# Moving one-hot products, GELU pairs and U steps in the first gate-table build of a one-core decoder trunk

## The reference

```python
q = (xn @ w_query).reshape(b, s, PEER_HEADS, 2, PEER_HALF)            # 8 heads, two halves of 128
sc = einsum('bshcd,hcnd->bshcn', q, sub_keys)                         # 128 keys per half
top_s, top_i = top_k(sc, 16)
best_s, best_pos = top_k(all 256 sums of two halves, 16)
expert_idx = top_i[..., 0] * 128 + top_i[..., 1]   # at best_pos
gates = softmax(best_s)
u = expert_u[ib]                                    # 128 experts of 1024 per token
act = gelu(einsum('ced,cd->ce', u, xb))
out = einsum('ce,ced->cd', gb * act, expert_v[ib])
```

## Time and profile before

| | |
|---|---|
| median of 3 runs | 2051.42 us (2044.77 to 2053.69) |
| the profiled execution | 2048.59 us, its span 2046.8 us |
| busy share of the span | PE 94%, DVE 59%, POOL 43%, ACT 20% |
| bytes moved | 613.47 MB, mean 300 GB/s |
| TensorE clock granted, mean | 0.96 of 2.4 GHz |

### The profile page before, as it was taken

How to read it: one execution, slowest core, us unless ns; L and a number is a source line. 1 busy time by engine, 2 the same in 40 slices (tenths; PEclk the granted TensorE clock), 3 DMA queues, 4 the chain that set the end, 5 groups by cost and what they waited for, 6 DMA issues and landing times.

```text
span 2046.8 us, 23875 instructions
## 1 busy us (share of the span) xinstructions
PE 1929.5 (94%) x8967; PEld 1246.4 (61%) x8967; DVE 1206.0 (59%) x3046; ACT 413.6 (20%) x963; POOL 878.3 (43%) x785
## 2 busy tenths in 40 slices
PE   8999999999989999999996789999999999999998
PEld 7688886956766787885675765444445543333332
DVE  1022101103968888889899999887777775444321
ACT  2233210111202454111211222000022320101102
POOL 0000000000855324445558355745566776666653
PEclk9999999999999999999998578999998999999999
DMA  7533444434999877999999587999998999999997
GB/s 236 151 117 114 146 153 145 143 108 137 378 334 397 282 250 251 379 386 379 332 358 387 192 264 241 409 409 409 409 384 321 347 332 405 409 409 409 409 382 285
DMA packets 252439, 613.47 MB, mean 300 GB/s; under 512 B 18676, under 2 KB 121124, under 8 KB 252324
## 3 DMA queue, kind: packets, MB, share of 16 engines
q0 software_dynamic: 110592, 402.70, 52.4%
q1 hardware_dynamic: 141120, 208.17, 29.4%
q10 hardware_dynamic: 612, 1.07, 0.2%
HBM read 609.77 MB, written 2.10 MB: 299 GB/s over the span
## 4 chain that ended last, share of the span: by engine, by line
PE 62%; DVE 13%; DMA 12%; POOL 7%; issue 3%; ACT 1%; another core or an unknown queue 1%; SPq 0%; DVEq 0%; ACTq 0%; POOLq 0%
PE ps L612 25%; PE ps L878 10%; PE ps L841 9%; DMA u_rows<-in_peer_u_dram,idx 8%; PE ps L627 7%; DVE u_rows L1353 5%; POOL u_rows L571 5%; PE ps L654 3%; PE ps L868 2%; POOL v_rows L585 2%; DMA wring<-in_w_branch_attn_dram 2%; DVE hot_a L1407 2%; DMA v_rows<-in_peer_v_dram,idx_turned 1%; DMA wring<-in_w_in_dram 1%
## 5 line engine op out<-in xcount | busy, mean ns | idle before, releaser
L571 POOL DMA_INDIRECT u_rows<-in_peer_u_dram,idx x512 | 591.5, 1155 | 979.0 <-DVE idx L1340 507.8
L1353 DVE CUSTOM_DVE_ANT_0 u_rows<-u_rows,xn 128x1024 f32<-128x1024 f32 x512 | 623.0, 1217 | 171.5 <-DMA u_rows<-in_peer_u_dram,idx 154.3
L612 PE MATMUL ps<-xT,wring 128*128 128x256 f32 x2432 | 552.7, 386 | 19.0 <-DMA wring<-in_w_in_dram 10.0
L612 PEld LDWEIGHTS ps<-xT,wring 128*128 128x128 f32 x2432 | 462.7, 193 | 87.8 <-DMA wring<-in_w_in_dram 10.8
L878 PE MATMUL ps<-d_rows,gates 128*128 128x512 f32 x1024 | 455.4, 598 | 0.5 <-issue 0.5
L878 PEld LDWEIGHTS ps<-d_rows,gates 128*128 128x128 f32 x1024 | 189.7, 190 | 265.2 <-issue 263.6
L841 PE MATMUL ps<-v_rows,diag 64*64 64x512 f32 x1928 | 260.0, 631 | 12.9 <-DMA v_rows<-in_peer_v_dram,idx_turned 7.9
L868 PEld LDWEIGHTS ps<-hot_b,hot_a 128*128 128x128 f32 x1024 | 148.2, 230 | 71.1 <-DVE hot_b L1415 36.5
L585 POOL DMA_INDIRECT v_rows<-in_peer_v_dram,idx x121 | 136.0, 1124 | 126.2 <-PE ps L841 92.3
L868 PE MATMUL ps<-hot_b,hot_a 128*128 128x64 f32 x1024 | 157.2, 318 | 33.4 <-DVE hot_b L1415 26.8
L841 PEld LDWEIGHTS ps<-v_rows,diag 64*64 64x64 f32 x1928 | 72.3, 138 | 158.5 <-issue 150.8
(11 more groups left out here) (197 smaller groups left out, 1701.2 us busy)
## 6 DMA issues: line engine op xcount, KB each, us to landing
wring<-in_w_in_dram SPq DMA_DIRECT2D x128, 512.0 KB
d_rows<-in_peer_v_dram SPq DMA_DIRECT2D x128, 512.0 KB
wring<-in_peer_w_query_dram SPq DMA_DIRECT2D x32, 512.0 KB
wring<-in_w_branch_conv_dram SPq DMA_DIRECT2D x16, 512.0 KB
wring<-in_w_branch_attn_dram SPq DMA_DIRECT2D x16, 512.0 KB
wring<-in_w_out_dram SPq DMA_DIRECT2D x16, 512.0 KB
wring<-in_xattn_wq_dram SPq DMA_DIRECT2D x16, 512.0 KB
wring<-in_xattn_wo_dram SPq DMA_DIRECT2D x16, 512.0 KB
```

The lines of the kernel that those rows point to most:

```text
L571: pool.indirect_dma_start(out=u_rows[:, n % URING, :], out_offset=None, in_=peer_u[0], in_offset=bass.IndirectOffsetOnAxis(ap=experts_of(g ...
L612: mm = pe.matmul(bank(job)[:, 0:HN], w[:, k % 4, P * b:P * (b + 1)], act[:, k, :], start=(k == 0), stop=(k == KT - 1))
L1353: dve.tensor_tensor_reduce(out=u, in0=u, in1=(xn2 if h else xn1)[:, i, :], scale=1.0, scalar=0.0, op0=ALU.mult, op1=ALU.add, accum_out=dot ...
```

## The change

The first 32 chunks stood in steps 268 to 302 (one to a step), with 22 V rows in steps 280 to 302. They now stand in steps 268 to 278, three to a step, with no V row. The blocks of the first half of the table stand in steps 281 to 390 (before 304 to 405), the second build in 392 to 427 with 76 V rows (before 407 to 433 with 84), and the steps up to 512 hold 140 V rows (before 110). In the first build `hot_a` of the ten chunks 2, 5, ..., 29 is written by ACT in two operations instead of by DVE: eight times the absolute value of the difference of iota and key, then relu of one minus it. The GELU chains of the groups 2k and 2k + 1 of half 0 run as one chain on 32 columns. `keep_running` lets PE repeat 4, 12 and 4 products of 128x512, whose result nobody reads, around the transposes of the tables.

```diff
-    CH_SLOT = spread(12, 46, 32) + spread(151, 177, 32)
-    BLK_SLOT = spread(48, 149, 64) + spread(179, 260, 64)
-    V_SLOT = (spread(24, 46, 22) + spread(48, 150, 14) + spread(151, 177, 84) + spread(179, 256, 110)
-              + spread(256, 280, 26))
+    CH_SLOT = spread(12, 23, 32) + spread(136, 171, 32)
+    BY_ACT = range(2, 32, 3)
+    BLK_SLOT = spread(25, 134, 64) + spread(173, 260, 64)
+    V_SLOT = spread(60, 134, 14) + spread(136, 171, 76) + spread(173, 256, 140) + spread(256, 280, 26)
-    ADD_SLOT = HSTEPS + 150
+    ADD_SLOT = HSTEPS + 135
+    def chain_of(g):
+        return g // 2 if g < HG else g - HG // 2
...
-        gl = tiny("gl", [P, 4, TOPK])
+        gl = tiny("gl", [P, 4, 2 * TOPK])
...
+            def keep_running(count):
+
+                for _ in range(count):
+                    pe.matmul(ps[:, 3, :], ident[:, :], xn2[:, 0, 0:BANK], start=True, stop=True)
+
             def table_transposes():
-                pe.wait_ge(wgt_rdy, HG)
+                pe.wait_ge(wt_done, 2 * SBH)
+                pe.wait_ge(x3_done, 2 * HT)
+                keep_running(4)
                 for b in range(NJB):
                     wait_taken(pe, NJOBS - 1 - b)
                 for i in range(HT):
                     for c in range(2):
-                        pe.transpose(ps[:, 6, P * (2 * i + c):P * (2 * i + c + 1)], e12[:, i, c, :], ident[:, :])
+                        mm = pe.transpose(ps[:, 6, P * (2 * i + c):P * (2 * i + c + 1)], e12[:, i, c, :], ident[:, :])
+                mm.then_inc(t_done, 1)
+                keep_running(12)
+                pe.wait_ge(wgt_rdy, HG)
                 for i in range(HT):
                     mm = pe.transpose(ps[:, 7, P * i:P * (i + 1)], wst[:, i, :], ident[:, :])
                 mm.then_inc(t_done, 1)
+                keep_running(4)
 
             def gate_chunk(ch):
                 pe.wait_ge(hot_rdy, ch + 1)
+                if ch in BY_ACT:
+                    pe.wait_ge(hot_steps, 2 * (BY_ACT.index(ch) + 1))
...
+            def first_hots(ch):
+                n = BY_ACT.index(ch)
+                i, o = 8 * ch // P, 8 * ch % P
+                if n == 0:
+                    act.wait_ge(t_out, 3)
+                    act.wait_ge(iotas, 2)
+                act.wait_ge(wb_done, ch - 1)
+                for t in range(8):
+                    ab = act.activation(hot_a[:, 8 * (ch % 2) + t, :], iota_a[:, :], ACT.Abs, scale=-1.0,
+                                        bias=e1T[:, i, o + t:o + t + 1])
+                ab.then_inc(hot_steps, 1)
+                act.wait_ge(hot_steps, 2 * n + 1)
+                a = hot_a[:, 8 * (ch % 2):8 * (ch % 2) + 8, :]
+                act.activation(a, a, ACT.Relu, scale=-1.0, bias=1.0).then_inc(hot_steps, 1)
...
-                if e == 5 and 0 < g <= GROUPS:
+                if e == 5 and 0 < g <= GROUPS and (g > HG or g % 2 == 0):
                     gelu_exp(g - 1)
...
+                for ch in BY_ACT:
+                    if CH_SLOT[ch] == tau:
+                        first_hots(ch)
                 for ch in range(CHUNKS):
                     if CH_SLOT[ch] + 1 == tau:
                         take_gates(ch)
...
-                dve.tensor_tensor(hot_a[:, 8 * (ch % 2):8 * (ch % 2) + 8, :],
-                                  e1T[:, i, o:o + 8].unsqueeze(2).to_broadcast([P, 8, P]),
-                                  iota_a[:, :].unsqueeze(1).to_broadcast([P, 8, P]), ALU.is_equal)
+                if ch not in BY_ACT:
+                    dve.tensor_tensor(hot_a[:, 8 * (ch % 2):8 * (ch % 2) + 8, :],
+                                      e1T[:, i, o:o + 8].unsqueeze(2).to_broadcast([P, 8, P]),
+                                      iota_a[:, :].unsqueeze(1).to_broadcast([P, 8, P]), ALU.is_equal)
```

More of the change, by code:

```diff
@@ L1060, in gelu_exp @@
             def gelu_exp(g):
-                act.wait_ge(gl_done, 7 * g + 4)
-                act.activation(gl[:, 2, :], gl[:, 1, :], ACT.Exp, scale=-GELU_C).then_inc(gle_done, 1)
+                n = TOPK * (1 + (g < HG))
+                act.wait_ge(gl_done, 7 * chain_of(g) + 4)
+                act.activation(gl[:, 2, 0:n], gl[:, 1, 0:n], ACT.Exp, scale=-GELU_C).then_inc(gle_done, 1)
             def diagonal(m):
@@ L1358, in gelu @@
                 hd, i, h = group(g)
-                r = g % GRING
-                a = dots[:, r, :]
-                n = 7 * g
+                first, wide = g - (1 - h), 2 - h
+                r = first % GRING
+                a = dots[:, r:r + wide, :]
+                s0, s1, s2, s3 = (gl[:, k, 0:wide * TOPK].rearrange("p (w e) -> p w e", w=wide) for k in range(4))
+                n = 7 * chain_of(g)
                 if part == 0:
                     dve.wait_ge(u_used, TOPK * (g + 1))
-                    dve.tensor_tensor(gl[:, 0, :], a, a, ALU.mult).then_inc(gl_done, 1)
+                    dve.tensor_tensor(s0, a, a, ALU.mult).then_inc(gl_done, 1)
@@ L1365, in gelu @@
                 elif part == 1:
                     dve.wait_ge(gl_done, n + 1)
-                    dve.tensor_scalar(gl[:, 0, :], gl[:, 0, :], 0.044715, 1.0, ALU.mult, ALU.add).then_inc(gl_done, 1)
+                    dve.tensor_scalar(s0, s0, 0.044715, 1.0, ALU.mult, ALU.add).then_inc(gl_done, 1)
                 elif part == 2:
                     dve.wait_ge(gl_done, n + 2)
-                    dve.tensor_tensor(gl[:, 1, :], gl[:, 0, :], a, ALU.mult).then_inc(gl_done, 1)
+                    dve.tensor_tensor(s1, s0, a, ALU.mult).then_inc(gl_done, 1)
@@ L1378, in gelu @@
+                    dve.reciprocal(gate_r[:, 0:wide], gate_s[:, r:r + wide]).then_inc(gl_done, 1)
                 elif part == 5:
-                    dve.wait_ge(gle_done, g + 1)
-                    dve.tensor_scalar(gl[:, 2, :], gl[:, 2, :], 1.0, None, ALU.add).then_inc(gl_done, 1)
+                    dve.wait_ge(gle_done, chain_of(g) + 1)
+                    dve.tensor_scalar(s2, s2, 1.0, None, ALU.add).then_inc(gl_done, 1)
                 elif part == 6:
                     dve.wait_ge(gl_done, n + 6)
-                    dve.reciprocal(gl[:, 2, :], gl[:, 2, :]).then_inc(gl_done, 1)
+                    dve.reciprocal(s2, s2).then_inc(gl_done, 1)
@@ L1386, in gelu @@
                     if h == 0:
-                        dve.scalar_tensor_tensor(out=wst[:, i, TOPK * hd:TOPK * (hd + 1)], in0=gl[:, 3, :],
-                                                 scalar=gate_r[:, g % 2:g % 2 + 1], in1=gl[:, 2, :],
-                                                 op0=ALU.mult, op1=ALU.mult).then_inc(wgt_rdy, 1)
+                        for k in range(HT):
+                            dve.scalar_tensor_tensor(out=wst[:, k, TOPK * hd:TOPK * (hd + 1)], in0=s3[:, k, :],
+                                                     scalar=gate_r[:, k:k + 1], in1=s2[:, k, :],
+                                                     op0=ALU.mult, op1=ALU.mult).then_inc(wgt_rdy, 1)
                     else:
@@ L1392, in gelu @@
                             to, a3, a2 = (t[:, k, :].rearrange("p (e two) -> p e two", two=2)[:, :, odd]
[L1393 removed]
+                                          for t, k in ((wgt, g - HG), (s3, 0), (s2, 0)))
                             ins = dve.scalar_tensor_tensor(out=to[p0.start + turn:p0.stop + turn, :], in0=a3[p0, :],
[L1395 removed]
+                                                           scalar=gate_r[p0, 0:1], in1=a2[p0, :],
                                                            op0=ALU.mult, op1=ALU.mult)
@@ L1458, in _ @@
                     dot(tau)
-                if 0 < g <= GROUPS and e < 8:
+                if 0 < g <= GROUPS and e < 8 and (g > HG or g % 2 == 0):
                     gelu(g - 1, e)
```

7 lines of the change are left out of this document (4 added, 3 removed).

## The result

The changed kernel takes 2111.23 us (median of 4 runs, 2108.27 to 2116.16) where the kernel before takes 2048.17 us (median of 4) beside it: ratio 1.0304, 95% interval 1.0274 to 1.0333. It is slower by 3%. The profiled execution took 2108.27 us, its span 2106.5 us.

A forecast was written before the change was run, and what follows sets the result against it. The prediction took transfers at 409 GB/s to bound most stages after the front, and DVE the first build. It summed 2048.6 + 57.7 (moved rows) + 24.5 (build) - 4 (repeats) - 1 (GELU pairs) to 2126 us, range 2078 to 2142.

The forecast's parts named there:

- What isn't carried in the build is paid later, 45 rows, +57.7.: Stages after the first build: 45 rows moved out of it cost 1.28 us each there, +57.7 us.
- the third rival: Second build: fewer V rows a step give back up to 32 us of its loss; chance of ending faster 0.05.
- The loop through ACT: First build: ACT's one-hots, bank emptying and PE's three chunks wait in a circle; build 164 us, +24.5 us.
- three chunks: PE's part of each round in the first build: 3 x 3.67 us at the lower clock.
- Round: First build, three chunks at the lower clock: 3.6 + 1.06 + 3 x 3.67 + 0.1 = 15.8 us.
- The lower clock: First build: PE stays at the lower clock, 3.67 us a chunk, against 1.9 at the full one.
- The 4 us that the repeats would give in the first round: First build's start: repeated products leave the first round partly at the full clock, -4 us.
- cost nothing: Ahead of the first build: the 20 repeated products, 18 us, fit where PE is idle and delay nothing.
- GELU pairs -1: Front: eight chains of about ten small DVE operations fewer, -1 us, bounds 0 and -2.
- The clock did not rise within a run of chunks: Rival for the first build: the clock rises within each run of chunks, total 2097 us; chance 0.17.
- DVE would bind at 88 us: Rival for the first build: the ACT loop doesn't close, DVE binds at 88 us, total 2054; chance 0.06.
- Break-even: First build: the change pays only if the build falls below 139.6 - 57.7 = 82 us.

The follow-up runs named there:

- e5_both: Changed kernel with banks emptied ahead of the one-hots on ScalarE and one repeated 128x512 product behind each of the 32 chunks; 2057.28 us, ratio 1.0040.
- e1_gates_first: Changed kernel with one edit: on ScalarE the banks of the step before are emptied ahead of the step's one-hots; 2085.27 us, ratio 1.0116.
- e2_dve_hots: Changed kernel with all 32 hot_a tiles of the first build made by VectorE again; 2081.82 us, ratio 1.0111.
- e8_again: The changed kernel as it is, measured once more on another chip; 2114.36 us, ratio 1.0327.
- e4_no_repeats: Changed kernel without the 4, 12 and 4 repeated products; 2126.34 us, ratio 1.0342.
- e7_pairs_only: Kernel before with the GELU pairs alone: old slots, no hot_a on ScalarE, no repeated products; 2046.02 us, ratio 0.9984.
- e6_old_slots: Changed kernel with the slots of the kernel before, keeping ten hot_a tiles on ScalarE, GELU pairs and repeated products; 2043.72 us, ratio 0.9963.

## Why the prediction was right

The time is in the range (2078 to 2142) and the sign and the mechanism are those forecast. The size came out smaller, 2111 for 2126. In the traces all three parts erred to the same side: the moved rows by 10.0 us, the build by 3.1 and its start by 4.4. By the steps:

- *What isn't carried in the build is paid later, 45 rows, +57.7.* Right in kind, measured +47.7 in the traces of before and after. The two dense stages took 52.0 of the forecast 56 (44 rows at 1.28 us), and the second build gave 4.3 back with one row more. That is the third rival in a small size; but it isn't firm: in the seven other traces with the same slots the stretch from step 392 to 433 took 171 to 182 us, where it took 169 here. e5_both and its build give 53 us, and the mean of all traces 51.5; the forecast is 5 to 6 us too high.
- *The loop through ACT.* Right: shown by e1_gates_first and e2_dve_hots. The forecast terms against the trace: eight operations with a pointer 2.45 (forecast 2.4), relu 1.06 (1.05 to 1.15), pause 4.63 (4.66), three chunks 10.47 (11.0). The last was mis-sized: a chunk in a run costs 3.49, since 3.67 includes its end. Round 15.1 for 15.8, build 157.0 for 164 less 4.
- *The lower clock.* Right: 0.51 in the build. The 4 us that the repeats would give in the first round did not come. In the profiled execution the clock fell with the first chunk. In that of e8_again three chunks ran at the full clock and gained 2 us, but "cost nothing" was wrong there: the repeats made DVE wait 2.2 us for the weights. e4_no_repeats has the same build without them.
- *GELU pairs -1.* The build began 5.4 us earlier. By e7_pairs_only the pairs are worth 3 us, with an interval from 8 us faster to 1 us slower; this term stays open. The front varies by more than 5.4 us from one execution to the next, so the early start is chance as far as these runs tell.
- The sum with the measured terms: 2048.6 + 47.7 + 17.4 - 5.4 = 2108.3, the profiled execution's own time. It must come out, since the three stretches make up the span; it is no further proof.
- *The rivals.* The clock did not rise within a run of chunks. In e2_dve_hots it stayed at 0.50 while PE was busy with chunks for 88.5 of 90 us. The rule of the Trainium skill (TensorE: Matmul & The Clock Gate, "What's actually happening"), that sustained activity opens the gate, would have made it rise; this trace contradicts it for these products. That DVE would bind at 88 us was right as a price and not as a forecast: e5_both, without the loop, has a build of 96.0 with DVE busy 90.6 and PE 90.5. Break-even was forecast at 82 us of build from the first one-hot; by the same count e5_both puts it at about 86, and the mean of the traces at 88.

The forecast wrote the old build's 139.6 us down to VectorE alone. e6_old_slots took 10 us of work off VectorE and, in its trace, less than 1 us off the build, so something else was all but binding too; TensorE at the lower clock is the likely one, but no run tests it alone.

## What to carry to other kernels

When an engine takes over a part of a producer's work, look at what is queued behind that part on it. Here ten operations that saved VectorE 1.1 us each closed a loop of 15 us a round, because they stood ahead of the emptying of a bank, and changing the order of two `for` loops in the code was worth 38 us. In a kernel that pays by the byte in most stages, a stage that doesn't fill the queue should be judged by its length less what it carries: shortening it by moving its rows out pays only beyond their price later.

## What the runs showed of the hardware

- Chunks of 128x64 products never brought TensorE's clock up by themselves: in e2_dve_hots PE was busy with them 88.5 of 90 us, and the granted clock stayed at 0.50 (1.2 GHz). In all fourteen traces, each rise of the clock in a first build came with V pairs, repeated products or dense blocks among the chunks just before it. With one 128x512 product behind each chunk the mean clock of the build was 0.95 (e5_both), and the chunk took 1.9 us instead of 3.5.
- A full clock handed to the chunks did not last. In e8_again the clock was 1.00 while the repeated products ran and for the first three chunks, 7.7 us with PE busy 5.8; in e2_dve_hots it was 1.00 for 7.2 us of chunks, with PE busy 5.95. Then it fell to 0.50, with only chunks on PE, and stayed there to the end of the build.
- ScalarE's operation of 128x128 with a pointer lasted 0.39 us, and eight in a row took 2.45 us, 0.29 from one start to the next, as the forecast's sum from 64 columns had given.
